# Loading the sample tokens' window keys on SyncE's queue, ahead of the value pages, instead of on GpSimd's queue

## The reference

```python
def nsa_sample(h, cache, j, win_buf, page_table, ...):
    q, q_rope, gates, rows, wrows = nsa_project(h, pos, w_in, q_norm, k_norm)
    ...
    wk = jnp.concatenate([win_buf, wrows], axis=1)       # 512 recent positions and the new one
    o = nsa_attend(q, q_rope, gates, pos, kc, vc, gather_sel, n_slc, wk[:, :, 0], wk[:, :, 1], ...)

def nsa_attend(...):
    p_cmp = masked_softmax(q . kc)                       # compressed branch
    o_cmp = p_cmp . vc
    top, idx = top_k(block score from p_cmp, 16)         # of 33 blocks of 64 positions
    o_sel = masked_softmax(q . k[selected]) . v[selected]
    o_win = masked_softmax(q . kw) . vw                  # window branch: the 512 recent keys and values
    return g0 * o_cmp + g1 * o_sel + g2 * o_win
```

## Time and profile before

| what | value |
|---|---|
| median of 3 runs | 4733.63 us (4728.02 to 4734.23) |
| profiled execution, its own time | 4735.88 us |
| its span, first to last instruction | 4734.1 us |
| mean granted TensorE clock | 0.908 of full speed |
| PE busy | 4030.9 us, 85% |
| DVE, ACT, POOL busy | 36%, 26%, 21% |
| first run of the changed stage | from about 800.5 us |
| second run of the changed stage | from about 4167 us |

### The profile page before, as it was taken

How to read it: one execution, slowest core, us unless ns; L and a number is a source line. 1 busy time by engine, 2 the same in 40 slices (tenths; PEclk the granted TensorE clock), 3 DMA queues, 4 the chain that set the end, 5 groups by cost and what they waited for, 6 DMA issues and landing times. The chain is left out here.

```text
span 4734.1 us, 79233 instructions
## 1 busy us (share of the span) xinstructions
PE 4030.9 (85%) x31852; PEld 3583.0 (76%) x31852; DVE 1713.0 (36%) x2487; ACT 1254.2 (26%) x2041; POOL 987.6 (21%) x745
## 2 busy tenths in 40 slices
PE   8669798599979728888799896999894879947999
PEld 7654586599978518887799884999894548837999
DVE  2358101233220464443433277332214840023332
ACT  3226111133210311122232134332222531112321
POOL 0324100033210022331233100332005340002330
PEclk9769898799989759998899997999996889978999
DMA  3200464522322010001223220323321025552232
GB/s 128 97 19 1 163 202 158 162 84 89 96 73 76 27 58 1 1 1 50 71 89 98 79 81 11 92 89 98 103 109 42 2 110 160 182 186 83 93 97 85
DMA packets 179737, 407.93 MB, mean 86 GB/s; under 512 B 40338, under 2 KB 96436, under 8 KB 178364
## 3 DMA queue, kind: packets, MB, share of 16 engines
q1 hardware_dynamic: 161028, 375.97, 24.4%
q10 hardware_dynamic: 13824, 16.78, 1.1%
q0 software_dynamic: 4672, 12.18, 0.7%
HBM read 388.22 MB, written 33.39 MB: 89 GB/s over the span
## 5 line engine op out<-in xcount | busy, mean ns | idle before, releaser
L252 PE MATMUL acc<-h_hi,ffn_w_lo 128*128 128x260 f32 x2816 | 799.1, 284 | 22.2 <-DVE ffn_w_lo L236 22.2
L252 PE MATMUL acc<-h_lo,ffn_w_hi 128*128 128x260 f32 x2816 | 801.9, 285 | 0.0
L252 PE MATMUL acc<-h_hi,ffn_w_hi 128*128 128x260 f32 x2816 | 798.7, 284 | 0.0
L252 PEld LDWEIGHTS acc<-h_hi,ffn_w_lo 128*128 128x128 f32 x2816 | 536.1, 190 | 24.9 <-DVE ffn_w_lo L236 24.9
L231 ACT ACTIVATE ffn_w_hi<-ffn_w_raw 128x1024 fp32r<-128x1024 f32 (+1 forms) x240 | 275.3, 1147 | 1031.1 <-PE acc L252 1031.1
L252 PEld LDWEIGHTS acc<-h_hi,ffn_w_hi 128*128 128x128 f32 x2816 | 534.7, 190 | 0.0
L252 PEld LDWEIGHTS acc<-h_lo,ffn_w_hi 128*128 128x128 f32 x2816 | 533.0, 189 | 0.0
L2504 PE MATMUL bh<-pages,cmp_w 128*128 128x256 f32 x2048 | 459.5, 383 | 47.0 <-DMA pages<-in_cache_kT 47.0
L236 DVE TENSOR_TENSOR ffn_w_lo<-ffn_w_raw,ffn_w_hi 128x1024 fp32r<-128x1024 f32 (+1 forms) x240 | 349.0, 1454 | 407.0 <-ACT ffn_w_hi L231 407.0
L2504 PEld LDWEIGHTS bh<-pages,cmp_w 128*128 128x128 f32 x2048 | 387.7, 192 | 110.9 <-DMA pages<-in_cache_kT 47.9
L252 PE MATMUL acc<-gu_lo,ffn_w_hi 128*128 128x260 f32 x1408 | 398.6, 283 | 0.0
(11 more groups left out here) (474 smaller groups left out, 7500.4 us busy)
## 6 DMA issues: line engine op xcount, KB each, us to landing
pages<-in_cache_kT SPq DMA_DIRECT2D x240, 384.0 KB, 3.8
ffn_w_raw<-in_w_gu SPq DMA_DIRECT2D x176, 512.0 KB, 3.7
ffn_w_raw<-in_w_down SPq DMA_DIRECT2D x64, 704.0 KB, 4.1
oT<-in_nsa_w_in SPq DMA_DIRECT2D x20, 1024.0 KB, 5.6
out_win_sample<-in_cache_win SPq DMA_DIRECT2D x2, 8176.0 KB
w<-in_rwkv_rkv SPq DMA_DIRECT2D x24, 512.0 KB, 3.6
conv_w_raw<-in_conv_w SPq DMA_DIRECT2D x24, 512.0 KB, 3.7
wk<-in_cache_wkT POOLq DMA_DIRECT2D x16, 512.0 KB, 10.4
```

Of the source, the lines that this page charges most:

```text
L252: mm = pe.matmul(out[:, a, 0:HALF], w[u][:, k, :], h[:, k0 + k, cols], start=(first and k == 0 and i == 0), stop=(last and k == kn - 1 and ...
```

## The change

The eight transfers of `wk` are issued by SP, before its loop over the tokens, and no longer by POOL, where only `before` is left. The semaphore `wk_in` is no longer one kept for POOL's transfers. Sizes, destinations and waits are unchanged.

```diff
-    wk_in, before_in = core.sig("nsv_wk_in", pool_dma=True), core.sig("nsv_before_in", pool_dma=True)
+    wk_in, before_in = core.sig("nsv_wk_in"), core.sig("nsv_before_in", pool_dma=True)
...
         @block.sync
         def _(sync):
+            for b in range(NB):
+                sync.dma_start(wk[:, b], io["cache_wkT"][j, b].rearrange("p g t n -> p g (t n)")).then_inc(wk_in.sem, 16)
             for b in range(1, NB):
...
         @block.gpsimd
         def _(pool):
             pool.dma_start(before[:], io["c_before"]).then_inc(before_in.sem, 16)
-            for b in range(NB):
-                pool.dma_start(wk[:, b], io["cache_wkT"][j, b].rearrange("p g t n -> p g (t n)")).then_inc(wk_in.sem, 16)
```

## The result

The changed kernel takes 4739.74 us (median of 20 runs, 4734.71 to 4747.34) against 4732.9 us before (20 runs, 4728.02 to 4736.52). The ratio is 1.0018, with a 95% interval from 1.0012 to 1.0025: 6 to 12 us slower. By the medians it is 6.8 us, by the means of the same runs 8.8. The forecast was +7.4 and 4741.0.

A forecast was written before the change was run, and what follows sets the result against it. SP's instruction stream was taken as the bound of each stage; eight wk issues add 3.7 us a stage, +7.4, everything else nothing, so 4733.63 + 7.4 = 4741.0 us, range 4732 to 4750.

The forecast's parts named there:

- The bound: In `nsa_sample_attend`, SP's instruction stream sends without a pause, 97 to 102 us a stage, and its last page sets the end.
- The eight issues: Added to SP at the stage's head, uncovered: 3.7 us a stage (2.8 to 4.6), +7.4 us for two stages.
- the stated spread: Issue cost (+5.6 to +9.2) and the page pace's 5.5 us together: +0.1 to +14.7, or 4733.7 to 4748.3 us.
- wk 5.4 us sooner: Window scores on PE start 5.4 us sooner, at about 814; worth nothing at the end, because SP's stream covers it.
- `before`, covered: POOL's `before` load now meets SP's 4 MB, but may come 9 us late for nothing, as DVE waits for window scores.
- The wait that grows: PE's waits for value pages grow by the 5.4 gained plus the 3.7 added, 9 us a stage; transpose at 908.
- this pace: SP's value-page issue period, 1.27 to 1.4 us a page; two equal streams in one run differ by 5.5 us.
- The rule of the Trainium skill: Several queues save only initiating time, "usually small relative to the DMA itself"; by it the sum would be 0, not +7.4.
- Rival A: Faster: the stage's end follows wk through ACT's pages or PE's path; 2 × −5.4 = −10.8, 4722.8 us; chance 0.07.
- Rival B: Slower: SP's sends stand until wk's backlog drains, 10.5 us a stage; +21, 4754.6 us; chance 0.10.
- Rival C: wk arrives no sooner, window scores stay at 819; the end is still SP's, +7.4 us; chance 0.08 within the forecast's.
- The Trainium skill's other rule: Simple loads belong on Sync, a path "generally faster"; by it the faster outcome, 4722.8 us, would follow.

The follow-up runs named there:

- the small loads: Against the kernel before, wk left on POOL, SP also issues eight 4 KB loads into a spare tile at the stage's head: 4743.2 us, 1.0018.
- the two-queue split: ACT, not SP, issues the second 8 pages of tokens 1 and 2: 4714.1 us from the kernel before (wk on POOL), 4702.9 from the changed one (SP).
- three queues: Against the two-queue split, of tokens 3 to 7 SP issues 4 pages, POOL 8, ACT 4: 4684.3 us with wk on SP, 4686.3 on POOL.
- 10 us fewer of issues: Against three queues with wk on SP, POOL's part cut from 8 to 4 pages for the last two tokens: 4685.5 us, 0.9902.

## Why the prediction was right, point by point

- **The bound.** SP's unbroken stream and its last page as the release of the end: shown by the small loads (+4.0 us on SP, as slow as the change) and by the four pages moved off it.
- **The eight issues, sized at 3.7 us, 2.8 to 4.6.** They took 4.09 and 4.07, 0.51 each: nearer to POOL's 0.52 than to the 0.46 of the loads of x. The term came to 8.2 us in the two stages instead of 7.4. That the total came within 0.6 us of the forecast by the medians is in part luck: by the means it is 8.8, the profiled stages grew by 10.6, and the stated spread of +0.1 to +14.7 reached almost down to no change.
- **wk 5.4 us sooner, worth nothing.** In the first stage it came 5.2 us sooner, the value products 6.0, and PE waited them off at token 2. Predicted were 814, 832.4 and 833.7 for the scores, the products and ACT's start; the trace has 814.20, 831.88 and 833.18.
- **`before`, covered.** DVE took it at 808.36 without a wait.
- **The wait that grows.** Expected were some 9 us a stage more of waiting for value pages; it was 10.5 in the first stage (43.0 after 32.5) and 5.6 in the second (43.5 after 37.9), where the value products started only 3.4 us sooner after the stage's start. The transpose was expected at 908 and came at 910.45: 0.4 us from the issue term, 1.7 from slower SP rows in that execution, 0.5 behind the last page. The forecast put this pace into its range, not its sum.
- **The rule of the Trainium skill** (DMA: Bandwidth & Descriptors, Issuing engines are not separate DMA queues), that another engine saves only the initiating time: by these runs so here, but this time isn't small beside the transfer. SP starts a value page of 0.13 MB every 1.27 us; by an estimate from the 0.40 MB/us of the full DMA engines, its bytes would pass in 0.33 us. The eight issues alone are 8.2 of the 10.6 us.
- **Rival A** (the end follows wk) is excluded for this kernel, and true in the two-queue split. The Trainium skill's other rule (DMA: Bandwidth & Descriptors, Issuing engine by pattern), that simple loads belong on Sync, gives the sign for that kernel only.
- **Rival B** (SP held by the backlog) is excluded: no wk issue took more than 0.74 us, and the next row began at once.
- **Rival C** (wk no sooner) is excluded here; with three queues it is nearly what happens.

## What to carry to other kernels

Ask of a transfer that you move not only when it will land but what its new queue is doing: on a queue that issues without a pause up to the end of a stage, each issue costs its time at the end, here 0.5 to 0.6 us, whether it carried 4 KB or 512 KB. A wait as visible as PE's 13 us for wk is worth nothing while a longer stream runs beside it, and becomes worth its length once that stream is shortened; so shorten the longest issue stream first, best by giving pages to an engine that only waits, and place the early load after that. Look before each further step whether the last consumer still waits for transfers: with three queues the DMA engines were full (1.02 to 1.07) and PE no longer waited for pages, and 10 us fewer of issues gained nothing.

## What the runs showed of the hardware

- An issue on SP cost the same for 4 KB and for 512 KB, both on 128 partitions: 4.01 and 4.05 us for eight. Loads of 256 KB cost more each, 0.56 us in a row of sixteen, and the first eight of them already 4.57 us. No run here tells why.
- A page load by a page number from memory has nearly the same period on three engines: in the first stage 1.26 to 1.27 us on SP and 1.22 to 1.28 on ACT, but for one row of 1.4 on each, and 1.32 to 1.41 on POOL (mean over 8 pages of a token), although POOL's bare issue is the longest (0.54 against 0.34).
- SP's rows in the second stage are slower than in the first in every kernel with the old split (the stream takes 102.4 against 96.9 us before, 106.7 against 102.6 after), with the same instructions and data sizes. No run here tells why.
- PE's idle time inside the products, for which the profile names no releaser, is 4.6 and 5.2 us in the two stages of the kernel before, where the DMA engines are 0.49 busy from 820 to 845 us, and 16 to 22 us a stage in the three-queue kernels, where they are 0.96 to 1.06 busy in that stretch. That the one causes the other is not shown.
